# The query projections one per step and TensorE's block work ahead of the value row

## What is computed

```python
def reference(x, positions, ..., w_gate_up_2, w_down_2):
    x = first_block(x, ..., peer_w_q, peer_sub_keys, peer_u, peer_v)
    return second_block(x, c_2, w_ada_2, ..., w_in_2, ..., w_out_2, w_gate_up_2, w_down_2)

# in first_block
x = x + peer_ffn(rms_norm(x, ffn_norm[l]), peer_w_q[l], peer_sub_keys[l], peer_u[l], peer_v[l])
# in second_block
hn = (_rms(x, norm1_g[l]) * (1 + sc1) + sh1).astype(x.dtype)
y = _mixer(hn, w_in[l], ...)        # starts with proj = hn @ w_in
x = x + g1 * (y.astype(x.dtype) @ w_out[l])
```

## Time and profile before

| | |
|---|---|
| median of 3 runs | 2663.78 us |
| the profiled execution | 2658.7 us, of which the span 2656.9 us |
| busy in the span: PE, DVE, POOL, ACT | 2101.0, 1728.9, 1033.2, 606.6 us |
| indirect gathers (queue q0) | 536.94 MB, 53.8% of the 16 DMA engines' span |
| other DMA (queue q1) | 138.13 MB, 15.6% |
| the PEER stage: first dot to last v row | 371.7 to 1990 us of the span |

### The profile page before, as it was taken

One profiled execution on the slowest core, in us unless ns is written; L12 is line 12 of the kernel. 1 busy time (PEld: TensorE's weight loads), 2 busy tenths in 40 slices (PEclk: granted clock), 3 DMA queues, 4 the chain that ended last, 5 costly groups with the idle time before them and its releaser, 6 DMA issues. The chain is left out here.

```text
span 2656.9 us, 25394 instructions
## 1 busy us (share of the span) xinstructions
PE 2101.0 (79%) x7625; PEld 1323.9 (50%) x7625; DVE 1728.9 (65%) x3556; ACT 606.6 (23%) x1394; POOL 1033.2 (39%) x1083
## 2 busy tenths in 40 slices
PE   4975857788765876775788777878787799799999
PEld 4954544444332334442344333333336774688877
DVE  4956338887877775567777587877847462544465
ACT  2134213342222111121212033222211230211121
POOL 0000015666666665566666466666750000000000
PEclk9985878989888988998999888888897897899999
DMA  5741038999999999899999899999984300333222
GB/s 176 288 143 64 17 127 300 357 341 364 355 337 409 356 369 360 303 355 359 371 402 403 318 371 347 361 364 331 380 326 151 112 10 0 111 95 95 79 79 95
DMA packets 266857, 676.48 MB, mean 255 GB/s; under 512 B 25725, under 2 KB 114162, under 8 KB 266738
## 3 DMA queue, kind: packets, MB, share of 16 engines
q0 software_dynamic: 147456, 536.94, 53.8%
q1 hardware_dynamic: 119282, 138.13, 15.6%
HBM read 672.87 MB, written 2.10 MB: 254 GB/s over the span
## 5 line engine op out<-in xcount | busy, mean ns | idle before, releaser
L2172 PE MATMUL bank<-arena 128*128 128x512 f32 x1536 | 816.1, 666 | 289.3 <-issue 120.6
L2402 DVE SCALAR_TENSOR_TENSOR arena<-arena,h_ps 128x1024 f32<-128x1024 f32 x512 | 612.5, 1216 | 175.8 <-DMA arena<-in_peer_u,arena 136.3
L2135 POOL DMA_INDIRECT arena<-in_peer_v,arena x512 | 511.4, 999 | 396.7 <-PE bank L2172 195.0
L2172 PEld LDWEIGHTS bank<-arena 128*128 128x128 f32 x1536 | 299.6, 209 | 640.0 <-issue 544.2
L2135 POOL DMA_INDIRECT arena<-in_peer_u,arena x512 | 506.6, 989 | 223.4 <-issue 143.5
L2415 DVE SCALAR_TENSOR_TENSOR x<-arena,x 128x1024 f32<-128x1024 f32 x128 | 164.5, 1285 | 48.0 <-DMA arena<-in_peer_v,arena 29.4
L1455 PE MATMUL bank<-hT,arena 128*128 128x256 f32 x512 | 134.7, 424 | 44.3 <-DMA arena<-in_peer_w_q 36.2
L2256 ACT ACTIVATE arena<-ident,arena 128x128 f32<-128x128 f32 x384 | 136.3, 394 | 78.1 <-PE bank L2172 36.1
L1455 PEld LDWEIGHTS bank<-hT,arena 128*128 128x128 f32 x512 | 109.4, 216 | 76.7 <-DMA arena<-in_peer_w_q 40.4
L142 DVE CAST parts<-arena 128x2048 fp32r<-128x2048 f32 (+4 forms) x60 | 68.1, 1136 | 112.1 <-DMA arena<-in_w_gate_up 72.7
L144 DVE TENSOR_TENSOR parts<-arena,parts 128x2048 fp32r<-128x2048 f32 (+4 forms) x60 | 126.7, 2111 | 4.5
(11 more groups left out here) (412 smaller groups left out, 3340.7 us busy)
## 6 DMA issues: line engine op xcount, KB each, us to landing
arena<-in_w_in SPq DMA_DIRECT2D x16, 1536.0 KB, 6.8
arena<-in_w_ada SPq DMA_DIRECT2D x12, 2048.0 KB, 9.7
arena<-in_w_gate_up SPq DMA_DIRECT2D x44, 512.0 KB, 5.0
arena<-in_peer_w_q SPq DMA_DIRECT2D x16, 1024.0 KB
arena<-in_w_down SPq DMA_DIRECT2D x22, 512.0 KB, 3.5
arena<-in_peer_u,arena POOLq DMA_INDIRECT x512
arena<-in_peer_v,arena POOLq DMA_INDIRECT x512
arena<-in_w_in SPq DMA_DIRECT2D x8, 1024.0 KB
```

What stands on the lines that cost most here:

```text
L2135: nc.gpsimd.indirect_dma_start(out=ring[:, n % R, :], out_offset=None, in_=a[table][0], in_offset=bass.IndirectOffsetOnAxis(ap=expert[:, s ...
L2172: ins = nc.tensor.matmul(psum[half][:, :], diag[:, m % R, :], v_ring[:, n % R, half * 512:(half + 1) * 512], start=(s % PH == 0 and j == 0 ...
L2402: nc.vector.scalar_tensor_tensor(out=u_ring[:, n % R, :], in0=u_ring[:, n % R, :], scalar=1.0, in1=h_ps[:, :], op0=ALU.mult, op1=ALU.mult, ...
```

## The change

PE's queue in each slot is reordered: `in_background` and `block2_pe` come first, the v row and the query after them. `query_due` gives the queries of tb 2 and 3 one to a step, in steps 12 to 19, with halves in slots 1 and 4 and scores in slot 6, as those of tb 0 and 1 have them. So bank 6 is in use for queries to step 19, when the second block's input projection has begun; the second block's early work therefore runs in three banks, 4, 5 and 7, in rotation. A tile's first token block takes the tile's slots 0 to 3 (two contraction pieces a slot), its second token block slots 4 to 7, each half in its own bank of the three, and ACT copies each half when it is done (two new semaphores, `in2_part` and `in2_half`). The gate rows move to banks 4 and 5, the transposes use the three banks. Tiles 8 and 9 wait for all eight tiles' copies. On SP's queue the load of tile 2 moves ahead of the load of query 15.

```diff
@@ -1442,9 +1442,7 @@
 
             if i < PH - 3:
                 return [(i + 3, 1)]
-            if 12 <= i < 16:
-                return [(PH + 2 * (i - 12), 0), (PH + 2 * (i - 12) + 1, 8)]
-            return []
+            return [(i - 12 + PH, 1)] if 0 <= i - 12 < PH else []
 
         def query(pe, Q, c):
             pe.wait_ge(w_q_loaded, 16 * Q + 16)
@@ -1533,6 +1531,7 @@
             return proj2_of[g][:, :, (t - 2) * 384:(t - 1) * 384]
 
         w_2_loaded, in2_summed, in2_copied = [sem("w_2_even"), sem("w_2_odd")], sem("in2_summed"), sem("in2_copied")
+        in2_part, in2_half = sem("in2_part"), sem("in2_half")
         gates_zeroed, bias_loaded, places_ready = sem("gates_zeroed"), sem("bias_loaded"), sem("places_ready")
         g_summed, g_copied = sem("g_summed"), sem("g_copied")
         r2_squared, r2_summed, r2_ready, r2_scaled = sem("r2_squared"), sem("r2_summed"), sem("r2_ready"), sem("r2_scaled")
@@ -1567,9 +1566,9 @@
             k0 = (0, KFOX + KML, KFOX)[i]
             sync.dma_start(w_out_a[i], w_out_all[:, k0:k0 + w_out_a[i].shape[1], :]).then_inc(w_out_loaded, 16)
 
-        def gate_rows(pe, g0):
+        def gate_rows(pe, g0, banks):
             for k in range(KD):
-                ins = nc.tensor.matmul(psum[6 + k // 4][:, k % 4 * P:k % 4 * P + P],
+                ins = nc.tensor.matmul(banks[k // 4][:, k % 4 * P:k % 4 * P + P],
                                        mod[:, g0 + k:g0 + k + 1].to_broadcast([P, P]), ident[:, :], start=True, stop=True)
             ins.then_inc(g_summed, 1)
 
@@ -1926,32 +1925,41 @@
         Y0 = U2 + 3 * UNITS + 6
         O2_0 = Y0 + 10
 
+        IN2_BANKS = [psum[4], psum[5], psum[7]]
+
+        def in2_bank(t, b):
+            return IN2_BANKS[(2 * t + b) % 3]
+
         def block2_pe(pe, slot):
             if slot == 1:
                 pe.wait_ge(b_copied, 2 * KD)
-                pe.wait_ge(sc_copied, 2 * PH)
-                gate_rows(pe, G1)
+                gate_rows(pe, G1, psum[4:6])
             if 6 <= slot < 6 + KD:
                 k = slot - 6
                 if k == 0:
                     pe.wait_ge(b_normed, 8)
-                if k == 2:
                     pe.wait_ge(g_copied, 1)
-                pe.wait_ge(b_copied, 2 * KD + max(k - 3, 0))
+                pe.wait_ge(b_copied, 2 * KD + max(k - 2, 0))
                 for b in range(2):
-                    ins = nc.tensor.transpose(psum[4 + k % 4][:, b * P:(b + 1) * P], rows[:, b, k * P:(k + 1) * P], ident[:, :])
+                    ins = nc.tensor.transpose(IN2_BANKS[k % 3][:, b * P:(b + 1) * P], rows[:, b, k * P:(k + 1) * P], ident[:, :])
                 ins.then_inc(b_turned, 1)
             t, k = (slot - I0) // KD, (slot - I0) % KD
             if 0 <= t < 10 and k == 0:
                 pe.wait_ge(w_2_loaded[t % 2], w_2_count(t))
                 if t == 0:
                     pe.wait_ge(b_copied, 3 * KD)
-                after(pe, in2_copied, t - 1)
+                after(pe, in2_copied, min(t - 1, 8) if t < 8 else 8)
+                if t == 9:
+                    pe.wait_ge(sc_copied, 2 * PH)
             if 0 <= t < 8:
-                n = TILES_2[t][1]
-                for b in range(2):
-                    ins = nc.tensor.matmul(psum[4 + t % 2 * 2 + b][:, 0:n], hT_of[0][:, k, b * P:(b + 1) * P], tile_2(t)[:, k, :],
-                                           start=(k == 0), stop=(k == KD - 1))
+                n, b = TILES_2[t][1], k // 4
+                if k == 4:
+                    after(pe, in2_half, t)
+                for kk in range(k % 4 * 2, k % 4 * 2 + 2):
+                    ins = nc.tensor.matmul(in2_bank(t, b)[:, 0:n], hT_of[0][:, kk, b * P:(b + 1) * P], tile_2(t)[:, kk, :],
+                                           start=(kk == 0), stop=(kk == KD - 1))
+                if k == 3:
+                    ins.then_inc(in2_part, 1)
             if t == 8:
                 for m in range(4 * k, 4 * k + 4):
                     part, kk = m // KD, m % KD
@@ -2003,21 +2011,22 @@
                 act.wait_ge(g_summed, 1)
                 act.wait_ge(b_normed, 6)
                 for i in range(2):
-                    ins = nc.scalar.copy(gate_row[:, i * 512:(i + 1) * 512], psum[6 + i][:, :])
+                    ins = nc.scalar.copy(gate_row[:, i * 512:(i + 1) * 512], psum[4 + i][:, :])
                 ins.then_inc(g_copied, 1)
             if 7 <= slot < 7 + KD:
                 k = slot - 7
                 act.wait_ge(b_turned, 2 * KD + k + 1)
-                nc.scalar.activation(hT_of[0][:, k, :], psum[4 + k % 4][:, 0:GT], ACT.Identity, scale=mod_gain[:, k:k + 1],
+                nc.scalar.activation(hT_of[0][:, k, :], IN2_BANKS[k % 3][:, 0:GT], ACT.Identity, scale=mod_gain[:, k:k + 1],
                                      bias=mod[:, SH1 + k:SH1 + k + 1]).then_inc(b_copied, 1)
-            t, k = (slot - I0) // KD - 1, (slot - I0) % KD
+            t, k = (slot - I0) // KD, (slot - I0) % KD
+            if 0 <= t < 8 and k == 4:
+                act.wait_ge(in2_part, t + 1)
+                nc.scalar.copy(proj2_dst(0, t)[:, 0, :], in2_bank(t, 0)[:, 0:TILES_2[t][1]]).then_inc(in2_half, 1)
+            t -= 1
             if 0 <= t < 10 and k == 0:
                 act.wait_ge(in2_summed, t + 1)
                 if t < 8:
-                    n = TILES_2[t][1]
-                    for b in range(2):
-                        ins = nc.scalar.copy(proj2_dst(0, t)[:, b, :], psum[4 + t % 2 * 2 + b][:, 0:n])
-                    ins.then_inc(in2_copied, 1)
+                    nc.scalar.copy(proj2_dst(0, t)[:, 1, :], in2_bank(t, 1)[:, 0:TILES_2[t][1]]).then_inc(in2_copied, 1)
                 else:
                     act.wait_ge(gates_zeroed, 2)
                     conv_load(act, 0, t - 8, psum[t - 3])
@@ -2120,7 +2129,9 @@
                             sync.dma_start(gate_bias[r0:r0 + n, col0:col0 + 1], a[name].rearrange("o n -> n o")).then_inc(bias_loaded, 16)
                         for t in range(2):
                             load_w_2(sync, t)
-                for t in range(2, len(TILES_2)):
+                    if Q == 2 * PH - 2:
+                        load_w_2(sync, 2)
+                for t in range(3, len(TILES_2)):
                     load_w_2(sync, t)
                 sync.dma_start(ml_gain_a, a["ml_h_g_2"].to_broadcast([P, ML_W])).then_inc(ml_gain_loaded, 16)
                 for i in range(3):
@@ -2225,6 +2236,8 @@
                     half_scores(pe, Q)
                 for i in range(STEPS + 1):
                     for j in range(PK):
+                        in_background(i * PK + j - B0)
+                        block2_pe(pe, i * PK + j - C0)
                         if i >= 1 and j not in DVE_J:
                             values(i - 1, j)
                         for Q, j0 in query_due(i):
@@ -2232,8 +2245,6 @@
                                 query(pe, Q, (j - j0) // 3)
                             if j == j0 + 5:
                                 half_scores(pe, Q)
-                        in_background(i * PK + j - B0)
-                        block2_pe(pe, i * PK + j - C0)
 
             @block.scalar
             def _(act):
@@ -2778,7 +2789,7 @@
 
             @block.tensor
             def _(pe):
-                gate_rows(pe, G2)
+                gate_rows(pe, G2, psum[6:8])
                 with pe.Fori(0, KF // 2) as i:
                     for odd in range(2):
                         pe.wait_ge(gu_split, 2 * i + odd + 1)
```

## The result

The changed kernel takes 2621.2 us (median of four runs, 2615.51 to 2636.86), the kernel before 2663.23 us in the runs beside it (four). The ratio is 0.9857, interval 0.9815 to 0.9899: faster by 1.0 to 1.9%. Two later repeats on other occasions gave 0.9873 and 0.9879. So the direction of the forecast was right, and its size, -13 us, about a third of what was measured, -32 to -38 us by the three ratios. The profiled execution took 2619.42 us (span 2617.6), 39 us less than the one of before.

A forecast was written before the change was run, and what follows sets the result against it. It took DMA bytes to bound most of the PEER stage, with steps 13 to 15 waiting for query weights. Terms -15 + 4 - 2 = -13 us gave 2650 us against the median; 8-in-10 range 2628 to 2672.

The forecast's parts named there:

- (a): Steps 12 to 19: one query a step removes weight stalls, leaving bytes at DMA share 0.98; -15 us, ends 2 and 23.
- the chain of 26.9 us through `w_q`: Steps 13 to 15: 12.3 us for a query's halves, then 14.6 until the next weights, through a single buffer.
- (b): Steps 16 to 19 take on a query each; PE stands 4 to 11 us for query 15's weights; +4 us, bounds 0 to 12.
- The forecast's own sign of being right: Steps 13 to 15 were to take 45 to 52 us each.
- (c): PE's block work ahead of the v row: 0 in steps with attention, -2 us in all for steps 19 to 21.
- Two rings of six gathers ... some 16 us: Gathers in flight, up to 6.3 MB or some 16 us at 384 GB/s, cover a late v row in attention steps.
- (d): Second block's three banks, half copies and moved waits cost nothing; step 22's stall for tile 8's weights stays.
- The slower one: Attention units, steps 0 to 8 and from 23: PE waits for ACT in each; +29 us, 2692 us; chance 0.11.
- bytes at 350 to 357 GB/s are the price: Steps 12 to 19: bytes, not waits, set the time, 416 to 424 us; total 2664 to 2672 us; chance 0.20.
- The fast one: Steps 12 to 19 run at 384 GB/s, the rate of steps 16 to 21, in 387 us; total about 2635; chance 0.19.

The follow-up runs named there:

- e4_two_buffers: Kernel before, still two queries a step in steps 12 to 15, plus a second query-weight buffer: 2628.07 us, ratio 0.9911 to before.
- e3_sp_order: Changed kernel with tile 2's load put behind query 15's again on SP's queue: 2621.18 us, ratio 0.9866 to before.
- e3_c: Repeat, all versions on one chip, of the changed kernel with tile 2's load behind query 15's: 2.9 us under the changed kernel beside it.
- e1_order: Kernel before with only PE's new order, block work ahead of v row and query: 2646.24 us, ratio 0.9985 to before.
- e2_spread: Changed kernel with PE's old order, v row and query ahead of block work: 2625.4 us, ratio 0.9893 to before.
- e5_ring5: Changed kernel with rings of five gathers instead of six, the diagonals' ring too: 2640.88 us, ratio 0.9945 to before.
- e6_half_bytes: Changed kernel gathering half of each row, 512 of 1024 elements, same number of gathers: 2595.56 us, ratio 0.9767 to before.
- e8_gates_step15: Changed kernel with tile 2's load behind query 15's and tile 8's tiny gate loads behind query 12's: 2517.81 us, ratio 0.9788 to before.
- e8_c: Repeat on a slower chip, tile 2's load behind query 15's and the tiny gate loads behind query 12's: 25 us under the changed kernel beside it.

## Why the prediction was right or wrong

**(a) was the step that failed, by its size.** Its mechanism was right: the chain of 26.9 us through `w_q` was seen, its stalls went, no wait for weights is left in steps 12 to 18, and `e4_two_buffers` shows that the chain alone was the cost. The term was sized wrongly: "what is left in steps 12 to 19 is the bytes" and "I take 0.98". It gave -15 us; steps 13 to 15 alone gave -41 (180.8 to 139.8). For all eight steps (a) and (b) together were to give -11, and gave -23 (-27 in both repeats). Without the wait of step 19 the eight steps took 385.4 and 381.1 us (`e3_sp_order`, `e3_c`): -31 and -35 where (a) had -15, beyond its best end of 23. The forecast's own sign of being right, steps 13 to 15 at 45 to 52 us each, held a gain of 25 to 45 us there and came nearly so (50.4, 44.5, 44.9); it could not tell the term from one twice its size.

Two things were wrong in it. Length times DMA share is not a fixed service time. It was 393.5 us in the kernel before, in 416.2 us at 357 GB/s; `e3_c` moved the same bytes in 381.1 us at 390 GB/s. The steps beside the stall, at 0.94 to 0.99 and 355 to 373 GB/s, were taken for full, and steps 14 and 15 made 405 and 404. And the share does not say what limits: half the bytes left steps 13 to 15 as long as they were. Bytes are a bound, but at 399 to 409 GB/s, and POOL's issuing is another close to it: 32 gathers at 1.24 us are 39.7 us a step, to which the other holds come. The earlier trace rows gave a better handle than the share: POOL stood 38.3 us for PE there, and most of that time came back. The rows above give -50.1 us of holds by PE, +4.6 "remote", +5.3 gaps, +1.9 for DVE and -2.6 busy time: -40.9, against -41.0 measured. But a removed hold is not paid one for one in general. Over the whole stage POOL's holds by PE fell by 78.2 us, from this row of before to 116.8,

```profile
POOL arena L2135 <- PE bank L2172: 195.0, 92, 18.5
```

and the stage only by 39.5: "remote" holds grew by 29.1 us, gaps by 14.5 and busy time by 5.5, while holds by DVE fell by 11.9.

The Trainium skill, page "DMA: Bandwidth & Descriptors", section "Where 436 GB/s comes from", has HBM bind at about 358 GB/s a core; the runs contradict that as a limit for this core, with 399 to 409 GB/s over whole steps. The same page of the Trainium skill, in its section on measured bandwidth, gives about 425 GB/s for a core that streams alone, which the rows approach and don't reach. The Trainium skill, page "Perfetto Trace Analysis", section "What "DMA-bound" means", holds that a kernel can be bound by the issuing engine's queue as well as by the DMA engines; here POOL's issue and gaps are 127.8 of 139.8 us, and the prediction did not weigh that reading.

**(b) was right in place, and too small.** The wait for `w_q` came where it was forecast, once, in step 19, 8.4 us in a range of 4 to 11, with the cause forecast: `e3_sp_order` takes it away. Its price was taken as +4, because a queue of gathers was thought to drain first. With the wait taken away step 19 is 8.1 us shorter (58.5 and 50.4; 59.9 and 50.8 in the repeats), so the wait cost 8 to 9 us: inside the bounds of 0 to 12, and twice what was taken. Steps 16 to 19 grew by 12 to 17 us in all, but the weights that moved there belong to (a). A DMA share of 1.03 was no cushion; what a stalled v row stops is POOL's issuing.

**(c) was right as far as can be told.** PE does ask for the results of ACT and DVE before they are there, and it costs nothing that shows. PE's waits in steps 0 to 10, total, times, longest, first in the kernel before (371.7 to 917 us), then in `e1_order` (371.6 to 917):

```profile
PE bank L2172 <- ACT arena L2256: 45.4, 16, 10.1
...
PE bank L1205 <- ACT hT L1196: 4.3, 1, 4.3
...
PE bank L1205 <- DVE arena L1142: 3.4, 1, 3.4
```

```profile
PE bank L1205 <- DVE arena L1139: 26.6, 4, 9.1
PE bank L1205 <- DVE arena L1142: 22.6, 6, 5.8
...
PE bank L1205 <- ACT hT L1196: 8.3, 5, 4.3
...
PE bank L2172 <- ACT arena L2256: 2.7, 3, 1.5
```

The wait for the diagonal at a step's first v row was 45.4 us and is 2.7: the block's work now runs in that gap. For it PE waits at the attention's own stages, 57.5 us in these rows instead of 7.7. One took the other's place, and steps 0 to 11 took 588.0 and 588.1 us. The waits are mainly for DVE, where the prediction named ACT. The gain of 2 us in steps 19 to 21 is too small to be seen, and `e1_order` and `e2_spread` leave room for 4 to 8 us that the order may bring elsewhere. "Two rings of six gathers ... some 16 us" as a cover was only argued, and `e5_ring5` speaks for a smaller one: with a place less (of the diagonals too) the kernel is 20 us slower.

**(d) was right.** Step 22 kept its stall, 20.7 us for 19.4, and no wait for a bank or a half copy appeared among the largest in steps 16 to 22.

**The rivals.** The slower one fell with `e1_order`: 2692 us was its figure, and the order alone gave 0.9985. That bytes at 350 to 357 GB/s are the price fell too: the eight steps made 379 and 390 GB/s, and `e6_half_bytes` did without half of them. The fast one, 2635 us, was the nearest, and still 14 us over: its 387 us for the eight steps, 391 with the 4 of (b), are near what the changed kernel took (393, 389, 389), but that is in part luck: its rate was too low (384 where `e3_c`, without the wait, made 390 GB/s) and its wait too cheap (4 us for 8 to 9), and the two errors nearly cancel. The time came out below the range.

**What stays open.** The ratios give -32 to -38 us, and steps 12 to 19 account for -23 to -27. Of the other 10 or so, steps 20 to 22 show 4 in the profiles; the order may have a few (`e2_spread`, not shown); the rest lies in steps whose work did not change and which scatter more than that: steps 0 to 11 took from 579.7 to 592.8 us in kernels that do the same there, not sorted by old and new. And POOL is held in most runs for about 2 us at a time by a semaphore change whose author the trace does not name ("remote"): 72.6 us in 36 holds before, 101.7 in 45 after, 105.0 in 53 with half the bytes. What they are was not found.

## What to carry to other kernels

Look at who holds the queue that issues a stretch's transfers, and take a removed hold's length as a rough ceiling of its price: other holds can grow in its place (41.0 us for 50.1 in steps 13 to 15, 39.5 for 78.2 over the stage). A DMA share near 1 says neither that the rate is at its end nor that bytes set the time; compare the rate with the best step of the trace, here 408 GB/s, and cut the bytes to see whether another bound stands beside them. A single buffer that is loaded only after its last use costs load plus use per item, wherever items come in pairs: spread the items, or add a buffer. Before a load is moved ahead of another in an in-order queue, work out when the second one is needed, and keep slow, tiny loads where nothing stands behind them.

## What the runs showed of the hardware

- An indirect gather of 128 rows occupies POOL's queue for 0.94 us and a gap of 0.30, whether the rows have 4 or 2 KB (means of 998 and 1001 ns for all v and u gathers with 4 KB, 1001 and 1005 with 2 KB).
- A drain on POOL behind such a gather takes 3.3 to 3.6 us, seen as idle time.
- The three tiny strided loads of the gates hold SP's queue for 22.3 to 22.5 us together, against 0.37 us for an issue that waits for nothing.
- One core's gathers, with and without loads beside them, reach 399 to 409 GB/s over whole steps; none of these runs showed more.
- Chips differ more than the change does: before took 2565.94 us on one and 2651.4 to 2663.23 on the others. On the fast one the profile of `e8_gates_step15` has no "remote" hold at all, on a slow one that of `e8_c`, the same kernel, has 89.7 us in 41. Its steps 24 to 27 took 41.8 us each, at 399 GB/s and a DMA share of 1.02.
